# Mixture-of-experts loop of a streaming encoder layer: one expert per loop turn instead of four, 16 KB weight pieces, row-packed combine

## The reference, cut to what matters

```python
def hier_moe(x2, ...):                      # x2: 320 x 2048, RMSNorm(h) * norm_ffn
    # router: group of 4, then the top 2 of its 8 experts, gate = product of probabilities
    def expert_block(args):
        rt, rg, e = args                    # token rows of this block, their gates, the expert
        xb = x_pad[rt]
        hb = jax.nn.silu(xb @ w_gate[e]) * (xb @ w_up[e])
        return (hb @ w_down[e]) * rg[:, None]
    ...
return h + ffn                              # then RMSNorm with norm_final
```

## Time and profile before

| | us |
|---|---|
| median of 3 runs | 1596.48 (1593.24 to 1598.14) |
| the profiled execution | 1594.92 |
| its span, first to last instruction | 1592.7 |
| PE busy | 1273.0 (80%) |
| DVE busy | 403.8 (25%) |
| ACT busy | 378.2 (24%) |

### The profile page before, as it was taken

How to read it: one execution, slowest core, us unless ns; L and a number is a source line. 1 busy time by engine, 2 the same in 40 slices (tenths; PEclk the granted TensorE clock), 3 DMA queues, 4 the chain that set the end, 5 groups by cost and what they waited for, 6 DMA issues and landing times.

```text
span 1592.7 us, 19699 instructions
## 1 busy us (share of the span) xinstructions
PE 1273.0 (80%) x7594; PEld 645.2 (41%) x7595; DVE 403.8 (25%) x752; ACT 378.2 (24%) x643; POOL 32.0 (2%) x41
## 2 busy tenths in 40 slices
PE   5999999999899998668668668659577766757765
PEld 5999998566556652112112112113122211212211
DVE  6354443245464351111101101102103011011113
ACT  5333232133333222112112112112110211211213
POOL 1000000000000000000000000000000000000000
PEclk9999999999899989889779789779887987887988
DMA  9445541121443279999999999999968999999993
GB/s 324 140 139 167 159 139 34 34 86 65 136 163 108 106 288 373 420 417 421 420 418 417 420 419 416 421 417 393 420 255 364 372 420 418 420 420 418 414 420 139
DMA packets 110802, 475.40 MB, mean 298 GB/s; under 512 B 14156, under 2 KB 51136, under 8 KB 60304
## 3 DMA queue, kind: packets, MB, share of 16 engines
q1 hardware_dynamic: 109776, 470.86, 74.5%
q0 software_dynamic: 832, 2.48, 0.4%
q10 hardware_dynamic: 64, 0.02, 0.0%
HBM read 469.96 MB, written 3.38 MB: 297 GB/s over the span
## 4 chain that ended last, share of the span: by engine, by line
PE 55%; DMA 34%; issue 6%; DVE 2%; ACT 1%; SPq 1%; ACTq 0%; DVEq 0%
DMA ring<-in_w_up 29%; PE ps L843 9%; PE ps L869 6%; PE ps L574 5%; PE ps L575 5%; PE ps L576 5%; DMA ring<-in_w_down 4%; PE ps L858 3%; PE ps L746 2%; PE ps L635 2%; PE ps L822 2%; PE ps L662 2%; PE ps L755 2%; PE ps L748 2%; PE ps L747 2%
## 5 line engine op out<-in xcount | busy, mean ns | idle before, releaser
L843 PE MATMUL ps<-ring,mix 128*32 128x512 f32 x2112 | 332.0, 742 | 241.5 <-DMA ring<-in_w_up 124.6
L843 PEld LDWEIGHTS ps<-ring,mix 128*32 128x32 f32 x2112 | 67.9, 123 | 485.7 <-issue 290.8
L1180 ACT COPY mix<-ps 128x512 f32<-128x512 f32 x33 | 35.2, 1066 | 568.4 <-PE ps L843 568.4
L574 PE MATMUL ps<-xT_hi,w_hi 128*128 128x320 f32 (+1 forms) x528 | 165.3, 313 | 3.3 <-DVE work L1274 3.3
L575 PE MATMUL ps<-xT_lo,w_hi 128*128 128x320 f32 (+1 forms) x528 | 164.5, 312 | 0.0
L576 PE MATMUL ps<-xT_hi,w_lo 128*128 128x320 f32 (+1 forms) x528 | 164.4, 311 | 0.0
L1549 DVE TENSOR_TENSOR mix<-mix,ps 128x128 f32<-128x128 f32 x33 | 9.5, 288 | 602.1 <-ACT mix L1183 602.1
L858 PE MATMUL ps<-ring,mix 128*32 128x512 f32 x1056 | 123.4, 599 | 31.5 <-DVE mix L1549 17.5
L1546 DVE TENSOR_TENSOR hreg<-ps,hreg 128x512 f32<-128x512 f32 (+1 forms) x120 | 81.9, 688 | 234.3 <-PE ps L869 227.0
L869 PE MATMUL ps<-mix 128*128 128x512 f32 (+1 forms) x216 | 105.2, 622 | 3.1 <-ACT mix L1188 3.1
L1288 DVE TENSOR_TENSOR w_lo<-ring,w_hi 128x1024 fp32r<-128x1024 f32 (+1 forms) x66 | 76.7, 1205 | 116.5 <-ACT w_hi L995 116.5
(11 more groups left out here) (262 smaller groups left out, 1131.1 us busy)
## 6 DMA issues: line engine op xcount, KB each, us to landing
ring<-in_w_gate SPq DMA_DIRECT2D x128, 1024.0 KB, 18.3
ring<-in_w_up SPq DMA_DIRECT2D x128, 1024.0 KB, 23.9
ring<-in_w_down SPq DMA_DIRECT2D x128, 1024.0 KB, 21.8
ring<-in_w_in SPq DMA_DIRECT2D x32, 1024.0 KB, 8.2
ring<-in_w_o SPq DMA_DIRECT2D x16, 1024.0 KB, 6.6
hreg<-in_x_prompt SPq DMA_DIRECT2D x4, 1024.0 KB, 6.4
ring<-in_w_uq SPq DMA_DIRECT2D x4, 768.0 KB, 4.8
ring<-in_w_uv SPq DMA_DIRECT2D x2, 1024.0 KB, 6.2
```

The lines of the kernel that those rows point to most:

```text
L574: pe.matmul(out, hi, xT_hi[:, c, :], start=c == 0, stop=False)
L843: last = pe.matmul(ps[r:r + B, 2, :], x[:, c + o, s, :], w[:, m, c + o, :], start=s == 0 and c == 0, stop=s == 3 and c == 2)
```

## The change

- **Loop.** 32 turns with one expert each. The down result `yb` (four column blocks of 32 rows under each other) is combined in the next turn: 12 units of 32 rows, each in a row group of its own (rows 32n to 32n+31 for features 512n onward), in the four banks 4 to 7. Four units stand behind both halves of `gate_up`, then the gather, then the other eight. The gates of each expert are transposed in its own turn.
- **Slots.** Slots 0 and 1 hold the first half of gate and of up, slots 2 and 3 the second; each slot is one DMA of 2 MB with 16 KB pieces. `gate_up` is called for two slots at a time, and slots are given back in stages: 0 with 1, 2 with 3, then 4, then 5.
- **Extra blocks** stand ahead of the main block's `down`, with banks and buffers of their own.
- **Picks** are made for one expert (32 columns) in place of four (128), the gates' picks apart from the tokens'.
- **Third tile** in `output`: its eight matmuls follow the chunks of a half, in place of two after every second chunk.
- **Layout of xn**: features are stored by (p c), so that a partition's 16 rows of gate and up are contiguous; the router now transposes the raw residual and its weights are scaled by `norm_ffn` once on DVE.

```diff
-                s = ring[:, i, :].rearrange("p (m c n) -> p m c n", m=2, c=4)
-                return [(s[:, m], w[512 * i:512 * i + 512, :].rearrange("(p c) n -> p c n", c=4))
-                        for m, w in enumerate((gate_w, up_w))]
-            s = ring[:, i, :].rearrange("p (c n) -> p c n", c=2)
-            v = down_w.rearrange("(p c) n -> p c n", c=4)
-            return [(s[:, c], v[:, 2 * (i - 4) + c, :]) for c in range(2)]
+                v = (gate_w, up_w)[i % 2].rearrange("(p c) n -> p (c n)", c=KC)
+                return ring[:, i, :], v[:, SLOT * (i // 2):SLOT * (i // 2 + 1)]
+            v = down_w.rearrange("(p c) n -> p (c n)", c=4)
+            return ring[:, i, :], v[:, SLOT * (i - 4):SLOT * (i - 3)]
 
...
                 for i in range(SLOTS):
-                    sp.wait_ge(weights_used, e * SLOTS + (i + 1 - SLOTS))
-                    sp.wait_ge(extra_used[i], used)
+                    stage = (0, 0, 1, 1, 2, 3)[i]
+                    sp.wait_ge(weights_used, e * 4 + (stage + 1 - 4))
+                    sp.wait_ge(extra_used[stage], used)
                     w = [a[k][0, bass.ds(e, 1)].rearrange("a b c -> (a b) c") for k in ("w_gate", "w_up", "w_down")]
-                    for dst, src in expert_slot(i, *w):
-                        sp.dma_start(dst, src).then_inc(slot_full[i], 16)
+                    dst, src = expert_slot(i, *w)
+                    sp.dma_start(dst, src).then_inc(slot_full[i], 16)
...
                             last.then_inc(o_used, 1)
-                        if j % 2:
-                            for k in range(2):
-                                last = pe.matmul(b[2][64 * k:64 * k + 64, :], mix[:, c - 1 + k, 256:320], w[:, j - 1 + k, :],
-                                                 start=half == 0 and j == 1, stop=final)
-                            if final:
-                                last.then_inc(psum_full, 1)
-                            elif j == 7:
-                                last.then_inc(wo_half_used, 1)
+                    for j in range(8):
+                        k = j % 2
+                        last = pe.matmul(b[2][64 * k:64 * k + 64, :], mix[:, 8 * (1 - half) + j, 256:320], w[:, j, :],
+                                         start=half == 0 and j < 2, stop=half == 1 and j > 5)
+                    last.then_inc(psum_full if half else wo_half_used, 1)
 
             def router_transpose(n, i):
                 tn = TILES[i][1]
-                pe.wait_ge(hg_ready, 3 * n + i + 1)
+                pe.wait_ge(drained["dve"], drain_count[f"wo{n}_{i}"])
...
-            def gate_up(x, s):
-
-                w = ring[:, s, :].rearrange("p (m c n) -> p m c n", m=2, c=4)
-                for c in (0, 2):
+            def gate_up(x, half):
+
+                w = ring[:, 2 * half:2 * half + 2, :].rearrange("p m (c n) -> p m c n", c=8)
+                for c in (0, 2, 4, 6):
                     for m in range(2):
                         for o in range(2):
                             r = B * (2 * m + o)
-                            last = pe.matmul(ps[r:r + B, 2, :], x[:, c + o, s, :], w[:, m, c + o, :],
-                                             start=s == 0 and c == 0, stop=s == 3 and c == 2)
+                            k = 8 * half + c + o
+                            last = pe.matmul(ps[r:r + B, 2, :], x[:, k % 4, k // 4, :], w[:, m, c + o, :],
+                                             start=half == 0 and c == 0, stop=half == 1 and c == 6)
                 return last
...
                     t0, tn = TILES[i]
-                    if u >= 3:
-                        pe.wait_ge(comb_added, added_before + (u - 2))
-                    pe.matmul(ps[0:tn, 5 + u % 3, :], gT[:, t0:t0 + tn], yg[:, 512 * n:512 * n + 512],
-                              start=True, stop=True).then_inc(comb_full, 1)
-
-            def combine_extra(x):
-
-                for i, (t0, tn) in enumerate(TILES):
                     for n in range(4):
                         if i:
-                            pe.wait_ge(x_added, x * 12 + (4 * (i - 1) + n + 1))
-                        rows = slice(B * n, B * (n + 1))
-                        pe.matmul(ps[0:tn, 4 + n, :], gTx[rows, t0:t0 + tn], yx[rows, :],
-                                  start=True, stop=True).then_inc(x_full, 1)
-
-            def extra_blocks(q, comb_before, e):
+                            pe.wait_ge(free_sem, base + (4 * i + n - 3))
...
-            with pe.Fori(0, NE // 4) as q:
-                comb_before = q * 12 + 13
-                for b in range(4):
-                    e = q * 4 + b
-                    pe.wait_ge(xg_ready, e + 1)
-                    for s in range(4):
-                        pe.wait_ge(slot_full[s], e * 32 + expert_count(s))
-                        gate_up(xg, s).then_inc(weights_used, 1)
-                        if b == 0:
-                            if s == 0:
-                                pe.wait_ge(y_copied, q * 4 + 1)
-                                pe.wait_ge(gt_copied, q + 1)
-                                drained_extra = pe.value_load(tables[0:1, 2, bass.ds(q * 4, 1)], min_val=12, max_val=12 * 64)
...
-                        pe.wait_ge(pick_ready, q + 2)
-                    cols = slice(B * ((b + 1) % 4), B * ((b + 1) % 4) + B)
-                    if b == 1:
-                        pe.wait_ge(gt_copied, q + 2)
-                    gather(pickr, cols, gathered)
-                    pe.wait_ge(h_copied, e + 1)
-                    fold(folded)
-                    pe.wait_ge(g_copied, e + 2)
-                    gathered_T(transposed)
-                    if b == 0:
-                        pe.wait_ge(gates_ready, q + 1)
-                        gates_T(gpick, P, gt_full)
-                    pe.wait_ge(hT_ready, e + 1)
-                    for s in (4, 5):
-                        pe.wait_ge(slot_full[s], e * 32 + expert_count(s))
-                        if s == 4 and b:
-                            pe.wait_ge(y_copied, e + 1)
-                        down(s).then_inc(weights_used, 1)
-                    extra_blocks(q, comb_before, e)
-
+            with pe.Fori(0, NE) as e:
+                added = e * 12 + 1
+                pe.wait_ge(xg_ready, e + 1)
+                for s in (0, 1):
+                    pe.wait_ge(slot_full[s], e * 16 + expert_count(s))
+                gate_up(xg, 0).then_inc(weights_used, 1)
+                for s in (2, 3):
+                    pe.wait_ge(slot_full[s], e * 16 + expert_count(s))
+                gate_up(xg, 1).then_inc(weights_used, 1)
+                pe.wait_ge(y_copied, e + 1)
+                pe.wait_ge(gt_copied, e + 1)
+                pe.wait_ge(comb_added, added)
+                drained_extra = pe.value_load(tables[0:1, 2, bass.ds(e, 1)], min_val=12, max_val=12 * 64)
+                pe.wait_ge(x_added, drained_extra)
+                combine((0,), gT, yb, (4, 5, 6, 7), comb_full, comb_added, added)
+                pe.wait_ge(pick_ready, e + 2)
+                gather(pickr, gathered)
+                combine((1, 2), gT, yb, (4, 5, 6, 7), comb_full, comb_added, added)
+                pe.wait_ge(g_copied, e + 2)
+                gathered_T(transposed)
+                pe.wait_ge(h_copied, e + 1)
+                fold(folded)
+                pe.wait_ge(gates_ready, e + 1)
+                gates_T(gpick, gt_full)
+                extra_blocks(e)
+                pe.wait_ge(hT_ready, e + 1)
+                for s in (4, 5):
+                    pe.wait_ge(slot_full[s], e * 16 + expert_count(s))
+                    down(hT, s).then_inc(weights_used, 1)
             pe.wait_ge(y_copied, NE + 1)
-            pe.wait_ge(comb_added, 12 * (NE // 4) + 1)
+            pe.wait_ge(gt_copied, NE + 1)
+            pe.wait_ge(comb_added, 12 * NE + 1)
             drained_extra = pe.value_load(tables[0:1, 4, NE - 1:NE], min_val=12, max_val=12 * 64)
             pe.wait_ge(x_added, drained_extra)
-            combine_units(range(12), 12 * (NE // 4) + 1)
...
-                    silu(silu_ready)
-                    copy_xT(xg, transposed, e + 2, xg_ready)
-                    if b == 0:
-                        act.wait_ge(gt_full, q + 1)
-                        act.copy(gT, ps[:, 0, 0:T]).then_inc(gt_copied, 1)
-                    act.wait_ge(weights_used, e * 6 + 6)
-                    copy_result([yg[B * b:B * (b + 1), 512 * j:512 * j + 512] for j in range(4)], y_copied)
-                    extra_blocks(e)
-
+            with act.Fori(0, NE) as e:
+                act.wait_ge(weights_used, e * 4 + 2)
+                copy_gate_up(h_copied)
+                copy_gathered(gathered, e + 2, g_copied)
+                copy_xT(xg, transposed, e + 2, xg_ready)
+                act.wait_ge(folded, e + 1)
+                silu(silu_ready)
+                act.wait_ge(gt_full, e + 2)
+                act.copy(gT, ps[:, 0, 0:T]).then_inc(gt_copied, 1)
+                extra_blocks(e)
```

(14 more changed lines are left out.)

206 lines of the change are left out of this document (98 added, 108 removed).

## The result

The changed kernel takes **1560.72 us** (median of four, 1560.03 to 1561.80) against 1595.93 us of the kernel before in the same comparison: ratio 0.978, with an interval of 0.976 to 0.980. Forecast were 1580 us, a move of 16.5 us from the 1596.48 that stood ahead. The profiled execution took 1561.32 us, its span 1559.2.

A forecast was written before the change was run, and what follows sets the result against it. DMA streaming weights, and its holes, was taken to bound the kernel. From a span of 1592.7 us, -13.5 (pieces), -3 (extra block), -7 (projection) and +7 (tail) gave 1576.2, forecast as 1580 us; range 1560 to 1625.

The forecast's parts named there:

- What bounds the kernel: Whole kernel: DMA streaming weights sets the end, 32 x 30.16 us, with two holes, the trunk ahead and the tail behind.
- Does PE's new turn fit: Expert loop: PE's new turn takes 24.6 us, 26.8 at the low clock, under 30, so the added work is hidden.
- The 6 us to spare: Expert loop: to the end of down PE needs 24 us, DMA has 30 us of loads, so DMA stays full.
- 16 KB pieces: Weight loads: doubling the piece saves 1.5%, 0.45 us an expert, -13.5 us in all (0 to -24).
- the rival in which the new body is fetched too: Expert loop: PE fetches its code anew every turn, 41 us a turn, some 1940 us; chance 0.20.
- Extra block: Extra block, now ahead of down: a hole of 22 us in place of 25.5, -3 us (-8 to +5).
- Output projection: Output projection: third tile in one batch saves 0.9 us in each of 8 halves, -7 us (0 to -9).
- First experts: Start of the expert loop: slots 0 to 3 free sooner, 4 and 5 unchanged; 0 us (-4 to +5).
- Tail: End of the kernel: last down +10 us, copies -1.7, last combine -1.3; +7 us in all (+4 to +10).
- Router: Router's part, with the scaling of its weights and the narrower picks: put at 0 (to -2).
- a turn of 31 us: Expert loop, rival of PE a little too long: slower adds, value loads and low clock, 1610 us; chance 0.08.

The follow-up runs named there:

- before_short_body: The kernel before, with PE's code of the extra block behind the fourth expert of a turn alone, not behind each of four: 1566.46 us, ratio 0.982.
- four_per_turn_pe: The changed kernel with PE's loop alone written out four experts to a turn, order of work unchanged: 1623.88 us, ratio 1.019.
- block_behind_gate_up: The changed kernel with fold right behind gate_up and the extra block right behind fold, ahead of combine and gather: 1570.56 us, ratio 0.985.
- down_first: The changed kernel with fold, a third of the combine and down ahead of the extra block, gather and remaining combine behind it: 1563.47 us, ratio 0.980.

## Why the prediction was off

- **What bounds the kernel**: right. DMA, and holes in it.
- **Does PE's new turn fit**: right. 11.9 to 12.6 us from `gate_up` to `down` for 13.4 (13.5 in the first turn), no fetch, 81% busy for 80%. The 0.8 us for a value load, which no row gave, don't show: L862 begins where `gate_up` ends. The 6 us to spare were between 3.7 and 8.3; in the trace the loads of slots 4 and 5 are issued 8 to 10 us before the slot ahead of them has landed.
- **16 KB pieces**, -13.5 us: 0.45 us an expert measured, and 13.1 us by the medians. The rows' line had 16 ns as the fixed part and would have given 24 us; that less would come was reasoned, how much less was a choice between 0 and 24, and that it met the digit is luck.
- **The step that failed** is one that isn't in the sum. The prediction read that q8 brought 12 pieces in each of seven turns and that PE stood 7, 4 and 5 us there, and used this to price the rival in which the new body is fetched too. In its own case, in which nothing is fetched from the second turn on, the end of the old body's fetches has no term and so counts nothing; the only reason near it is "A change of PE's work counts only if it makes holes or fills them." The steady loop did hide most of PE's stalls. It didn't behind the extra block, where DMA waited for PE, and the pieces of code themselves share the weights' engines. Taken out alone the fetches are worth 27.5 us, more than the whole forecast; by the ledger the span falls by 30.3 us, 9.0 in the period, 19.5 in what is lost above it and 1.8 ahead of the second expert.
- **Extra block**, -3 us: the wrong sign. The 25.5 us that served as the price of the hole before had PE's stalls in them: reckoned in the same way over the same 100 us, before_short_body loses 12.6. The changed kernel loses 30.0, where 22 were forecast. Main block to `gates_T` took 1151.94 - 1139.55 = 12.4 us for 12.2 and the picks 2.9 for 3; so the first hole was as forecast, 22.4 us. The missed term is slots 4 and 5, which come free only 24 us behind the others and make a second one, of 3.3 us; the last 4 us or so are a lower rate around the two. Against the old loop this is 14 us lost. By the ledger the two kernels' losses are 32.3 and 29.9 us, 2.4 apart, which looks like the forecast's 3: two errors, of 19.5 and 17.1 us, that nearly cancel.
- **Output projection**, -7 us: right in its mechanism, 9.0 in the stage and 10.6 in all. Within the stage the term was mis-sized by the batch's start, 1.1 us a half for 0.9.
- **First experts**, 0: the second expert is in 14.6 us earlier, 11.0 of it from the earlier start of the first `gate_up` (576.38 for 587.41), so -3.6, within -4 to +5. Other kernels with the changed loads and trunk have it from 612 to 617, so a part of that is chance.
- **Tail**, +7 us: 6.4. The last `down` starts at 1530.79, 6.8 us behind the last weights at 1523.95, for 6.
- **Router** 0 to -2: 0 to -1.

Two slips in its sums changed nothing. A body of 692 instructions is 44 KB, 2.7 pieces of 16 KB, and can touch four at most, not five. And a turn of 31 us in place of 29.7 would give 1580 + 1.3 x 31 = 1620 us, not 1610.

Step by step the runs go from the kernel before to the changed one as 27.5 (code: 1593.98 to 1566.46) + 23.0 (pieces, projection and router: 1566.46 to 1543.49) - 17.2 (the new loop: 1543.49 to 1560.72) = 33.3 us, against 35.2 measured. This path closes by its making, up to the 1.9 us by which the two comparisons' times of the kernel before differ, and its steps depend on their order: the code is worth 27.5 us on the old loads and 31.1 on the new ones. The independent check is the middle step, for which pieces (13.1) and projection (10.6), measured alone on the changed kernel, give 23.7.

The rival in which the code is fetched in each turn did not happen. four_per_turn_pe shows that its mechanism is real: at 20 us of stalls for four experts it costs 63 us. Its other half, that the kernel before was that case, was in the rows already.

## What to carry over

When a loop is bound by DMA, look at the queue of instructions before and after a change of its body: if the body outgrows what the engine keeps, each turn fetches it, and stalls that look covered can be paid where the stream is already dry. Price what a change removes from the profile with the same care as what it may add. And a hole in a stream of loads has several ends, one for each group of buffers: freeing one group earlier can just move the hole to the next, as it did in block_behind_gate_up and down_first.

## What the runs showed of the hardware

- A packet of 4, 8 or 16 KB costs 9.4 ns more than its bytes, in a straight line: periods of 30.72, 29.82 and 29.37 us for 12.58 MB. Some 8.5 ns of it are the packet's own and the rest each DMA's. At no fixed part the period would be 28.92 us, 435 GB/s; that is the line's estimate.
- A DMA into 64 neighbouring partitions runs at half the rate, 216 against 429 GB/s, with the engines busy to 100.8%: a packet of 16 KB takes 1.22 us in place of 0.61.
- A 16 KB piece of PE's code takes 1.03 us (mean, four_per_turn_pe) on the engines on which a packet of weights of that size takes 0.62.
- PE kept loop bodies of 692, 1,384 and 1,502 instructions and refetched 2,549 and 2,770. The limit lies between 1,502 and 2,549.
- Sixteen products with the third tile's 64 columns cost 3.7 us in one batch, and 4.8 us in four groups between products of 128 columns.
